# Two mixers reordered: head 0 first, convolution inputs among heads 0 and 1, layer norm in head 6, gated convolution outputs in head 7

## The reference, cut to what matters

```python
hx = modulate(rmsnorm(x, norm1_g[i]), sx1, ax1)
px = hx @ w_in[i]                    # conv a | conv g | q | k | v | gate logits
# 8 heads, each with two softmax maps over all keys:
s = einsum('bqhcd,bkhcd->bhcqk', q, keys) * scale
p = softmax(s, -1);  w = p[:, :, 0] - lam * p[:, :, 1]
out = rmsnorm(w @ vals, sub_g) * (1.0 - lam_init)
# convolution branch, 512 channels:
z = a * sigmoid(g)                                # "gated pair" of blocks
z = depthwise_conv(z, w_dw, 31 taps) + b_dw
y_conv = silu(layernorm(z, ln_g, ln_b)) @ w_conv_out
# merge
g_conv, g_attn = split(sigmoid(gate_logits + b_gate))
x = x + gx1 * ((g_conv * y_conv + g_attn * (attn @ w_attn_out)) @ w_out)
```

## Time and profile before

| what | value |
|---|---|
| median of 3 runs | 2612.6 us |
| profiled execution | 2616.48 us, its span 2614.7 us |
| TensorE matmul busy | 2367.3 us (91%) |
| VectorE, ScalarE busy | 1389.5 us (53%), 1069.2 us (41%) |
| granted TensorE clock, mean | 0.945 |
| mixer 3, first block to the first gate after head 7 | 1068.8 to 1518.1 us |
| mixer 4, the same | 2036.8 to 2338.8 us |

### The profile page before, as it was taken

The page is one execution under the profiler, slowest core; times in us unless marked ns, Lnnn a source line. Parts: engine busy times, 40 slices in busy tenths (PEclk is TensorE's granted clock), DMA queues, the critical chain, the costliest instruction groups (busy, mean ns, idle before and its releaser), DMA issues.

```text
span 2614.7 us, 34654 instructions
## 1 busy us (share of the span) xinstructions
PE 2367.3 (91%) x13646; PEld 1878.6 (72%) x13646; DVE 1389.5 (53%) x2341; ACT 1069.2 (41%) x1838; POOL 33.4 (1%) x40
## 2 busy tenths in 40 slices
PE   5798899999888999879979899899999788988999
PEld 2466677777666888656658677588888666868999
DVE  4154423333565444788763534544345887555665
ACT  4154421212454333435554532423323546554543
POOL 0300000000010000000000000000000000000000
PEclk8899999999998999889989889899999889989999
DMA  6810434443324777325502122332222211325454
GB/s 260 289 42 33 144 130 154 136 153 121 138 65 161 261 255 242 121 81 194 186 29 86 56 71 88 123 106 97 88 98 101 84 57 53 110 73 178 146 186 145
DMA packets 94880, 335.87 MB, mean 128 GB/s; under 512 B 10624, under 2 KB 12672, under 8 KB 94464
## 3 DMA queue, kind: packets, MB, share of 16 engines
q1 hardware_dynamic: 94720, 333.67, 37.1%
HBM read 332.58 MB, written 1.05 MB: 128 GB/s over the span
## 4 chain that ended last, share of the span: by engine, by line
PE 77%; DVE 10%; ACT 5%; DMA 4%; issue 3%; SPq 0%; ACTq 0%; DVEq 0%
PE out L1036 22%; PE out L1037 21%; PE out L1038 21%; DMA raw<-stream 4%; DVE stage L1650 3%; PE sc L1016 2%; PE pv L1123 2%; PE sc L1101 2%; DVE w_lo L1391 1%; PE pt L1111 1%; PE aux L1046 1%; ACT e_t L1297 1%; ACT w_hi L1157 1%; DVE smax L1596 1%; PE pt L1016 1%
## 5 line engine op out<-in xcount | busy, mean ns | idle before, releaser
L1036 PE MATMUL out<-act_hi,w_lo 128*128 128x512 f32 (+1 forms) x2272 | 813.6, 358 | 57.4 <-DVE act_lo L1550 45.1
L1037 PE MATMUL out<-act_lo,w_hi 128*128 128x512 f32 (+1 forms) x2272 | 793.9, 349 | 0.0
L1038 PE MATMUL out<-act_hi,w_hi 128*128 128x512 f32 (+1 forms) x2272 | 791.4, 348 | 0.0
L1157 ACT CAST w_hi<-raw 128x1024 fp32r<-128x1024 f32 (+2 forms) x444 | 452.5, 1021 | 487.0 <-PE out L1038 434.0
L1391 DVE TENSOR_TENSOR w_lo<-raw,w_hi 128x1024 fp32r<-128x1024 f32 (+2 forms) x444 | 528.0, 1194 | 202.9 <-ACT w_hi L1157 202.5
L1036 PEld LDWEIGHTS out<-act_hi,w_lo 128*128 128x128 f32 x2272 | 442.4, 195 | 149.3 <-issue 86.1
L1038 PEld LDWEIGHTS out<-act_hi,w_hi 128*128 128x128 f32 x2272 | 441.4, 194 | 53.3
L1037 PEld LDWEIGHTS out<-act_lo,w_hi 128*128 128x128 f32 x2272 | 442.7, 195 | 50.4 <-issue 0.5
L1036 PE MATMUL out<-mix_hi,w_lo 128*128 128x256 f32 (+1 forms) x1184 | 403.5, 341 | 3.1 <-DVE mix_lo L1623 1.7
L1037 PE MATMUL out<-mix_lo,w_hi 128*128 128x256 f32 (+1 forms) x1184 | 399.4, 337 | 0.0
L1038 PE MATMUL out<-mix_hi,w_hi 128*128 128x256 f32 (+1 forms) x1184 | 398.9, 337 | 0.0
(11 more groups left out here) (160 smaller groups left out, 1732.8 us busy)
## 6 DMA issues: line engine op xcount, KB each, us to landing
raw<-stream SPq DMA_DIRECT2D x604, 512.0 KB, 3.9
raw<-stream SPq DMA_DIRECT2D x16, 384.0 KB, 4.1
raw<-stream SPq DMA_DIRECT2D x16, 256.0 KB, 3.2
x<-xin SPq DMA_DIRECT2D x1, 2048.0 KB, 11.3
consts<-const SPq DMA_DIRECT2D x1, 1344.0 KB, 9.3
x<-ctx SPq DMA_DIRECT2D x1, 1024.0 KB, 5.8
out<-x SPq DMA_DIRECT2D x8, 128.0 KB, 1.7
consts<-const SPq DMA_DIRECT2D x1, 320.0 KB, 11.1
```

The source lines that it names most:

```text
L1036: nc.tensor.matmul(ps, wl, xh, start=(k == 0), stop=False)
L1037: nc.tensor.matmul(ps, wh, xl, start=False, stop=False)
L1038: ins = nc.tensor.matmul(ps, wh, xh, start=False, stop=(k == s.nk - 1))
L1157: nc.scalar.copy(w_hi[:, number % HL, 0:n], raw[:, place[number] % RAW, 0:n]).then_inc(S["hi_ready"], 1)
```

## The change

The steps of both mixers are put in another order. Head 0's k and q blocks come first and are interleaved (k with 512 columns, q with 512 or 256). Gated pairs 0 and 1 follow inside head 0's preparation, with 8 taps after each; pairs 2 and 3 go into the last groups of heads 0 and 1. Taps are spread up to the first group of head 6. The layer norm goes to head 6. Each group of head 7 gets products of the convolution output: group m does the gate block of tile m and the product of tile m-1; the last product stands after head 7. The layer norm's result has buffers of its own, `conv_hi` and `conv_lo`, with a semaphore `conv_ready`, so `s.mix_free` goes. The `ada` steps are spread over all heads (6, then 5 each). The kernel object is made with a smaller reserved scratch area in SBUF, 1024 bytes per partition.

```diff
-        s.src_ready = after("act_ready" if src == "act" else "mix_ready")
+        s.src_ready = after({"act": "act_ready", "mix": "mix_ready", "conv": "conv_ready"}[src])
...
-                t = min(range(len(glu)), key=lambda t: (taps_done[t], t))
-                if taps_done[t] == CONV_K:
+                left = [t for t in range(len(glu)) if glu[t].role == "glu" and taps_done[t] < CONV_K]
+                if not left:
                     break
+                t = min(left, key=lambda t: (taps_done[t], t))
...
-        for t in range(4):
+        def conv_gate(t):
             g = w("w_cg", t, n, "sg", func=ACT.Sigmoid)
             g.qg, g.qg_free = take("sgl", 2, None)
-            a = w("w_ca", t, n, "glu", other=g, free=last.get(("cz", 0)))
-            if t == 0:
-                together(g, a)
-            last["sgl", g.qg] = a.rel
-            glu.append(a)
-            conv_taps(8)
+            glu.append(g)
+
+        def conv_value(t):
+            g = glu[t]
+            glu[t] = w("w_ca", t, n, "glu", other=g, free=last.get(("cz", 0)))
+            last["sgl", g.qg] = glu[t].rel
...
-                s.mix_free = None if h < 4 else ("wb_done", state["yconv_end"])
...
         def gated_conv(m):
             def go():
-                product(gate(m), "w_conv_out", m, 4, 4, "yconv")
-                state["yconv_end"] = len(blocks)
+                if m:
+                    product(conv_gates[m - 1], "w_conv_out", m - 1, "conv", 4, "yconv")
+                if m < KD:
+                    conv_gates.append(gate(m))
...
-        for f in head_work(0):
-            f()
-            conv_taps(4)
+        q_block, k_block, q_norm, q_done, v_block, k_norm, k_done, v_turn = head_work(0)
+        k_block()
+        q_block()
+        together(held["k", 0], held["q", 0])
+        q_norm()
+        v_block()
+        q_done()
+        k_norm()
+        conv_pair(0)
+        k_done()
+        v_turn()
+        conv_taps(8)
+        conv_pair(1)
+        conv_taps(8)
...
-                          [total, v_turn], [scale], [low]]
+                          [v_turn, total], [scale], [low]]
...
-                          [total, v_turn, scale, low]]
-            if both and h == 4:
-                groups[4].append(conv_mean)
-                groups[5].append(conv_centre)
-                groups[6].append(conv_squares)
+                          [v_turn, total, scale, low]]
+            if h < 2:
+                if both:
+                    groups[6].append(lambda h=h: conv_gate(2 + h))
+                    groups[7].append(lambda h=h: conv_value(2 + h))
+                else:
+                    groups[3].append(lambda h=h: conv_pair(2 + h))
+            if both and h == 6:
+                groups[1].append(conv_mean)
+                groups[2].insert(0, conv_centre)
+                groups[3].append(conv_squares)
                 groups[7] += [conv_rstd, conv_scale]
-            if not both and h == 4:
+            if not both and h == 6:
                 groups[1].append(conv_mean)
                 groups[2].insert(0, conv_centre)
                 groups[2].append(conv_squares)
-                groups[3] = [total, v_turn, scale, conv_rstd, low, conv_scale]
-            if h == 5:
...
-            ada_now = ada_left[:10]
+                groups[3] = [v_turn, total, scale, conv_rstd, low, conv_scale]
+            if h == 7:
+                per = KD // len(groups)
+                for m in range(KD):
+                    groups[m // per].append(gated_conv(m))
+            ada_now = ada_left[:5 if h else 6]
...
-                slots = (4 - h) * len(groups) - j + (4 if both else 1)
+                slots = (6 - h) * len(groups) - j + 1
...
         square()
+        gated_conv(KD)()
         total()
...
+        conv_hi = sb("conv_hi", [P, 4, NT], F32R)
+        conv_lo = sb("conv_lo", [P, 4, NT], F32R)
...
-                        for g in group:
-                            assert g.n <= s.n and g.nk == s.nk
+                        for g in group:
+                            assert g.nk == s.nk
+                            xh = hi[:, s.k0 + k, 0:g.n]
+                            xl = lo[:, s.k0 + k, 0:g.n]
...
-    nc = bacc.Bacc("TRN2", target_bir_lowering=False, num_devices=1)
+    nc = bacc.Bacc("TRN2", target_bir_lowering=False, num_devices=1, dynamic_dma_scratch_size=1024)
```

More of the change, by code:

```diff
@@ L580, in taps_due, with conv_pair @@
             return left if slots == 1 else max(0, -(-(left - 2 * 3 * slots // per_head) // slots))
-        for t in range(4):
+        def conv_gate(t):
             g = w("w_cg", t, n, "sg", func=ACT.Sigmoid)
             g.qg, g.qg_free = take("sgl", 2, None)
-            a = w("w_ca", t, n, "glu", other=g, free=last.get(("cz", 0)))
-            if t == 0:
-                together(g, a)
-            last["sgl", g.qg] = a.rel
-            glu.append(a)
-            conv_taps(8)
+            glu.append(g)
[3 more added lines that the diff above has]
+            last["sgl", g.qg] = glu[t].rel
+        def conv_pair(t):
+            conv_gate(t)
+            conv_value(t)
         state = {}
@@ L619, in conv_scale @@
             signal("ln_h", 4)
-            finish_mix(s, 4)
-            last["y", 0] = s.mix
+            last["y", 0] = signal("conv_ready", 4)
         def gate(tile):
@@ L626, in gate, with product @@
             return g
-        def product(g, mat, m, k0, nk, role):
-            y = wb(layer, mat, m, "mix", k0, nk, n, role, other=g)
+        def product(g, mat, m, src, nk, role):
+            y = wb(layer, mat, m, src, 0, nk, n, role, other=g)
             if role == "yattn":
@@ L730, in layer_second @@
                 groups[2].append(conv_squares)
-                groups[3] = [total, v_turn, scale, conv_rstd, low, conv_scale]
-            if h == 5:
-                if both:
-                    for m in range(KD):
-                        groups[4 + m // 4].append(gated_conv(m))
-                else:
-                    groups[2] += [gated_conv(m) for m in range(5)]
-                    groups[3] = [gated_conv(m) for m in range(5, 8)] + groups[3]
-            ada_now = ada_left[:10]
+                groups[3] = [v_turn, total, scale, conv_rstd, low, conv_scale]
[4 more added lines that the diff above has]
+            ada_now = ada_left[:5 if h else 6]
             ada_left = ada_left[len(ada_now):]
             for j, g in enumerate(groups):
-                slots = (4 - h) * len(groups) - j + (4 if both else 1)
+                slots = (6 - h) * len(groups) - j + 1
                 if slots > 0:
@@ L762, in layer_second @@
                 gates.append(gate(KD + m))
-            y = product(gates[m], "w_attn_out", m, 0, KD, "yattn")
+            y = product(gates[m], "w_attn_out", m, "mix", KD, "yattn")
             y.by_k = m == 0
@@ L933, in build @@
             o_squared ox_ready ox_hi ln_sum ln_sq ln_x ln_h s_done ln_done vec_in cond_in x_in const_in ctx2_in small_in stored
-            silu_ready turn_ready turn_read dve_seq act_seq pool_seq bank_zero lam_ready sum_exp q_guess q_norm""".split()
+            silu_ready turn_ready turn_read dve_seq act_seq pool_seq bank_zero lam_ready sum_exp q_guess q_norm conv_ready""".split()
         S = {n: ctx.enter_context(nc.semaphore(n)) for n in names}
@@ L991, in _ @@
         def _(pe):
-            seen = {"act": 0, "mix": 0}
+            seen = {"act": 0, "mix": 0, "conv": 0}
             def need(src, name, value):
@@ L1019, in _ @@
                 elif s.kind == "wb" and (s.mate is None or s.number < s.mate.number):
-                    hi, lo = (act_hi, act_lo) if s.src == "act" else (mix_hi, mix_lo)
+                    hi, lo = {"act": (act_hi, act_lo), "mix": (mix_hi, mix_lo), "conv": (conv_hi, conv_lo)}[s.src]
                     group = [s] if s.mate is None else [s, s.mate]
@@ L1317, in _ @@
                     act.wait_ge(S["ox_ready"], s.x[1])
-                    wait(act, s.mix_free)
                     nc.scalar.activation(mix_hi[:, s.h, 0:s.n], o_rows[s.slot][:, 0:s.n], ACT.Copy, scale=col(s.layer, "og")).then_inc(S["ox_hi"], 1)
@@ L1329, in _ @@
                         link(nc.scalar.activation(b, b, ACT.Silu, scale=col(s.layer, "ln_g", t), bias=col(s.layer, "ln_b", t)))
-                        nc.scalar.copy(mix_hi[:, 4 + t, 0:s.n], b).then_inc(S["ln_h"], 1)
+                        nc.scalar.copy(conv_hi[:, t, 0:s.n], b).then_inc(S["ln_h"], 1)
                 elif s.kind == "merge":
@@ L1681, in zlo @@
                         dve.wait_ge(S["ln_h"], s.h0 + t + 1)
-                        nc.vector.tensor_tensor(mix_lo[:, 4 + t, 0:s.n], z_sq[:, t, 0:s.n],
-                                                mix_hi[:, 4 + t, 0:s.n].bitcast(F32), ALU.subtract).then_inc(S["mix_ready"], 1)
+                        nc.vector.tensor_tensor(conv_lo[:, t, 0:s.n], z_sq[:, t, 0:s.n],
+                                                conv_hi[:, t, 0:s.n].bitcast(F32), ALU.subtract).then_inc(S["conv_ready"], 1)
```

3 lines of the change are left out of this document (1 added, 2 removed).

## The result

The changed kernel takes 2592.8 us (median of 4 runs, 2587.1 to 2594.4) against 2611.4 us before, measured beside it; the ratio is 0.9923, 95% interval 0.9895 to 0.9951. It is 18.6 us faster, where 46.6 were forecast (2612.6 to 2566).

A forecast was written before the change was run, and what follows sets the result against it. TensorE was taken as the bound, busy 91% of the span, so only its waits and lower clock could be won. Gains of 30 (mixer 3) and 17 us (mixer 4) gave 2566 us, range 2544 to 2603.

The forecast's parts named there:

- lost time: The prediction's measure for a stretch: its length less PE busy times PEclk; 88.7 us in mixer 3, 62.9 in mixer 4.
- Part 1: Beginning to end of head 0: 16 us lost for 28.4 in mixer 3, gain 12; mixer 4 gains 8.
- Part 2: Heads 1 to 5: more taps make VectorE equal to TensorE; costs 7 us in mixer 3, 2 in mixer 4.
- Part 3: Layer norm in head 6: 21.6 us lost for 31.7 in mixer 3, gain 10; mixer 4 loses 1.
- Part 4: Head 7 with gates and products: lost time falls to 2.5 us in each mixer, gaining 15 and 12.
- the rival that VectorE paces the heads: Heads limited by VectorE: gain 27 us, 2586; if the beginning is no better either, 7, 2606; chance 0.20.
- 2 at the lower clock: Head 0 of mixer 3: 2 us lost to lower clock after TensorE's 6 us wait for the first exponentials.
- 2 in the rest of head 0: Head 0 of mixer 3: a further 2 us lost after the first exponentials' wait and its lower clock.
- The rule on the table loads: Both mixers: 1.28 us per load, six on the path; the skill's 2.66 per switch would give 2574.
- The signs: Head 0's scores 30 us sooner, then 6 us wait; heads 2-5 35-37 us, VectorE over 0.88; head 7 waits under 3.

The follow-up runs named there:

- Taps first: Changed kernel with each group's taps issued ahead of its blocks instead of behind them: 2565.9 us, ratio 0.9834.
- the kernel with only head 7: Kernel before with only the convolution outputs moved into head 7 on buffers of their own: 2586.8 us, ratio 0.9912.

## Why the prediction was wrong

**The sum.** 47 us were forecast in the two mixers and 22.6 of lost time went. The mixers are shorter by 19.6; the other 3.0 lie in PE busy times PEclk (2.0 in mixer 3, 1.0 in mixer 4), which should not have moved for the same matmuls, so the measure is good to some 3 us. Of the 24.4 that are missing, 10.2 lie in Part 1 in mixer 3, 9.3 in Part 2 (4.3 in mixer 3, 5.0 in mixer 4) and 4.8 in Parts 3 and 4 of mixer 4. The time lies in the range, between the two values of the rival that VectorE paces the heads, 2586 and 2606, but the runs show VectorE's order more than its pace.

**Part 1 failed, in mixer 3.** It was to win 12 and won 2.2. The wait that it forecast is there: the first exponentials came 6.86 us late, for 6. The step that failed is what I put behind that wait, "2 at the lower clock" and "2 in the rest of head 0": head 0 lost 17.7, not 10. (The other 2.5 of the 10.2 are the stretch ahead of head 0, 8.5 for 6.) TensorE's timeline in head 0 after:

```profile
1127.84 2.08 PE L1126 MATMUL sc<-k_t,q_t 64*128 64x512 f32 x4 [6.86 <-ACT e_t L1322]
1132.83 1.12 PE L1136 MATMUL pt<-consts,e_t 128*128 128x128 f32 x4 [2.91 <-DVE e_t L1639]
...
1136.73 0.63 PE L1062 MATMUL out<-act_lo,w_hi 128*128 128x512 f32 x1
...
1141.44 0.39 PE L1062 MATMUL out<-act_lo,w_hi 128*128 128x512 f32 x1
```

and the busy times of two stretches there:

```profile
1128.00:1134.00 6.00, 3.09 (x10) 1.51 (x11) 5.23 (x8) 1.87 (x5) 0.00 (x0) 0.50 0.46 173
1134.00:1140.50 6.50, 6.50 (x19) 5.43 (x20) 5.72 (x13) 3.86 (x10) 0.00 (x0) 0.50 0.02 5
```

Behind the 6.86 the transposes waited another 2.91 for the normalization, with two taps ahead of it. Through both stretches the granted clock is 0.50, the 1.2 GHz level; the 9.6 us that TensorE was busy there lose half, 4.8, where I had counted 2. Mending the order of the taps does not bring the part back by itself: then the new beginning is worth 0 to 4 us in both mixers together, by medians. The stalls ahead of head 0 were paid for VectorE's taps, and the same taps are paid for in heads 0 to 3. What does bring it back is to take the second eight taps off the way to the first maxima as well: beginning and head 0 then lose 12.7, under the 16 of the forecast, and the heads take these taps for 2.0. (The old beginning without its last taps was not run, so what the new one is worth then is open.) In mixer 4 the part came as forecast by its own measure, 14.2 for 14.

**Part 2 was too small, by the place of the taps more than by their number.** For heads 2 to 5 of mixer 3 I had 16.4 lost and lengths of 36.5, 35.5, 35 and 35; they lost 16.8 at 35.9, 37.1, 35.4 and 35.3. That is luck: the reason that I gave was half of VectorE's idle time left over by a nearly full engine, with a share over 0.88. It is 0.85 in all four: VectorE had time and spent it waiting for `w_hi`, with the taps still to come. Head 1 lost 5.9 for 2, and mixer 4's heads 16.7 for 11.7. I had read the taps' count and price from the trace, and not where they stand in VectorE's queue; the earlier trace rows shows only those ahead of head 0, directly ahead of the maxima, and not those behind a weight subtraction. Taps first lowers heads 1 to 5 of mixer 3 to 14.5 lost, by the same measure, from 22.7, and those of mixer 4 to 5.9 from 16.7. With the taps first the kernel takes 2565.9 us, as forecast, but that too is in part luck: its heads lose less than forecast, and its beginning and head 0 in mixer 3 lose 20.1 for 16.

**Part 3 came nearly as forecast** in mixer 3, 23.4 for 21.6, with its two waits at head 7's start at 4.8 and 1.5 us (forecast 3.33 and 3.8). Moving the chain ahead in head 6 wins nothing, so there the price is the chain and not its place. In mixer 4 the part lost 21.0 for 18; of its two waits at head 7's start one is the layer norm's, 4.7 us, and the other, 3.9, is for a gate's bank, as in Part 4.

**Part 4 held in mixer 3 and failed in mixer 4.** Head 7 of mixer 3 loses 0.6 for 2.5 with PEclk at 1.00. Alone the part gains 23 to 25 of the forecast 27, but the sum hides a miss: by the profile of the kernel with only head 7 mixer 3 gained 20.2 for 15 (14.4 where both kernels have the taps first), and mixer 4 gained 3.0 for 12 (4.8). In mixer 4 the rest of head 7 loses 4.3 for 2.5 after, and the whole of head 7 lost 9.8 where no layer norm stood ahead of it. For mixer 4 I had put 2.5 without a working. The table loads, 18 more as counted (42 for 24), did not come back on TensorE in mixer 3, as its 0.6 us show. In mixer 4 they did in part: without Sigmoid its head 7 is 5.0 us shorter.

**The rule on the table loads.** The rows of after have the next activation 1.30 us behind the start of a load of 1.28, as the earlier trace rows do. The Trainium skill, "ScalarE: Activation LUTs", section "What ACT_TABLE_LOAD costs", puts a switch at 2.66 with a drain; no drain shows: a load with work on both sides, at 1428.25 us, starts 0.02 us behind the instruction before it, and the next activation 1.30 us behind the load's start. Taking 32 loads away wins 8 us in all. By the page the time would have been 2574, and the one measured is above that too, but for the reasons above. What the loads cost is lost where one stands between a wait and the work that waits: loading ahead of the wait wins 11, with the taps first.

**The signs.** Of those that I had named, head 0's scores came 32.6 us sooner, the wait was 6.86, heads 2 to 5 took 35 to 37 us, and head 7 had no wait over 3 us behind its start; only VectorE's share was off. Except for the heads' lengths, which came out by luck, they sat on terms that held, and none sat on the rest of head 0 or on the normalization.

## What to carry to other kernels

Filler work on an engine that takes its queue in order can cost more by its place than by its amount (here 23 us against some 13): put it directly behind the instruction after which the engine would wait anyway, and ahead of the step that waits. When work is moved out of a stall of that engine, ask first where the same work then runs; a stall removed there can be paid again bit by bit. A forecast by stretches should be checked in each mixer by itself, since a good sum can hide a miss, as in Part 4. And a load of tables belongs ahead of a wait, not between it and the work.

## What the runs showed of the hardware that was not expected

Waits of one to two microseconds of TensorE cost more than themselves. In mixer 4, heads 3 and 4 after show a PEclk of 0.94 and take 27.4 and 27.0 us, with waits of 2.19 and 1.49 us in the one and 2.07 and 1.10 in the other. In the taps-first kernel these two heads have waits of 3.3 us together, 3.5 less, and take 24.3 and 24.1 us at a PEclk of 1.00, 6.0 less. In head 0 of mixer 3 the waits of 6.86 and 2.91 us left the clock at 0.50 until 1140.5, and a matmul of a weight block took 0.63 us there for 0.39.
